# Mixer of the second block: an order of its own for VectorE, and the gates' chain as two events

## What is computed

```python
h = modulate(rms_norm(x, g_norm1), shift1, scale1)
proj = h @ w_in                                # 1024 -> 3088 columns
sb_q, sb_k, sb_v, gq, gk, gv, gg, gf = split(proj)
o_sb = stick_breaking_attention(sb_q, sb_k, sb_v)      # 8 heads of 64
log_alpha = log_sigmoid(gf @ w_fg2 + b_fg2) / 16
o_gla = gla_chunk_causal(gq, gk, gv, log_alpha)        # 4 heads, chunks of 64
o_gla = rms_norm_by_head(o_gla) * g_gla_out * silu(gg)
x = x + (1 + gate1) * (concat(o_sb, o_gla) @ w_out)
```

## Time and profile before

| | |
|---|---|
| median of 3 runs | 1524.2 us (1524.11 to 1524.61) |
| the profiled execution's own time | 1521.82 us |
| its span, first to last instruction | 1520.0 us, mean granted PE clock 0.981 |
| PE busy | 1474.6 us, 97% |
| DVE busy | 785.1 us, 52% |
| ACT busy | 550.4 us, 36% |
| loads of raw weights, 1024 KB each | 5.2 us from issue to landing |
| the mixer | about 851 to 1100 us |

### The profile page before, as it was taken

One profiled execution on the slowest core, in us unless ns is written; L12 is line 12 of the kernel. 1 busy time (PEld: TensorE's weight loads), 2 busy tenths in 40 slices (PEclk: granted clock), 3 DMA queues, 4 the chain that ended last, 5 costly groups with the idle time before them and its releaser, 6 DMA issues.

```text
span 1520.0 us, 18225 instructions
## 1 busy us (share of the span) xinstructions
PE 1474.6 (97%) x6646; PEld 1194.9 (79%) x6646; DVE 785.1 (52%) x1013; ACT 550.4 (36%) x699; POOL 25.2 (2%) x48
## 2 busy tenths in 40 slices
PE   6999999999999999999999888999999999999997
PEld 5887888888888888888888756666677888888886
DVE  7345454566456444544645645454456653563564
ACT  4343212223224422323143514334535542552342
POOL 1000000000000000000000000000000000000000
PEclk8999999999999999999999899999999999999999
DMA  5323544334432334253432211110122232323221
GB/s 174 110 85 119 171 163 155 124 109 169 165 111 83 111 125 152 84 172 103 131 105 83 83 56 56 56 56 28 56 83 83 89 105 83 110 87 107 83 83 55
DMA packets 135789, 158.18 MB, mean 104 GB/s; under 512 B 2513, under 2 KB 129071, under 8 KB 135743
## 3 DMA queue, kind: packets, MB, share of 16 engines
q1 hardware_dynamic: 129024, 131.08, 26.6%
q0 software_dynamic: 6240, 26.30, 5.2%
q10 hardware_dynamic: 479, 0.17, 0.0%
HBM read 155.44 MB, written 2.10 MB: 104 GB/s over the span
## 4 chain that ended last, share of the span: by engine, by line
PE 93%; DVE 3%; ACT 2%; issue 1%; DMA 1%; SPq 0%; ACTq 0%; DVEq 0%
PE bank L437 29%; PE bank L439 28%; PE bank L438 28%; ACT weights_hi L785 1%; PE aux L717 1%; DMA gates<-in_x 1%; PE aux L459 1%; PE aux L741 1%; DVE weights_lo L1116 1%; PE aux L472 1%; PE bank L717 1%; PE aux L652 0%; PE aux L727 0%; PE aux L547 0%; PE aux L506 0%
## 5 line engine op out<-in xcount | busy, mean ns | idle before, releaser
L437 PE MATMUL bank<-operand_hi,weights_hi 128*128 128x512 f32 x1936 | 766.4, 396 | 8.3 <-DVE operand_lo L1128 5.6
L438 PE MATMUL bank<-operand_lo,weights_hi 128*128 128x512 f32 x1936 | 756.8, 391 | 0.0
L439 PE MATMUL bank<-operand_hi,weights_lo 128*128 128x512 f32 x1936 | 756.6, 391 | 0.0
L437 PEld LDWEIGHTS bank<-operand_hi,weights_hi 128*128 128x128 f32 x1936 | 365.8, 189 | 93.4 <-issue 17.5
L439 PEld LDWEIGHTS bank<-operand_hi,weights_lo 128*128 128x128 f32 x1936 | 365.4, 189 | 77.3
L438 PEld LDWEIGHTS bank<-operand_lo,weights_hi 128*128 128x128 f32 x1936 | 366.0, 189 | 75.2 <-issue 1.2
L1116 DVE TENSOR_TENSOR weights_lo<-raw,weights_hi 128x1024 fp32r<-128x1024 f32 (+1 forms) x244 | 296.0, 1214 | 166.9 <-ACT weights_hi L785 161.3
L785 ACT ACTIVATE weights_hi<-raw 128x1024 fp32r<-128x1024 f32 (+1 forms) x244 | 253.6, 1045 | 300.1 <-PE bank L439 300.1
L790 ACT ACTIVATE operand_hi<-value 128x512 f32 (+1 forms) x88 | 55.7, 633 | 125.6 <-DVE value L1304 34.0
L1126 DVE TENSOR_TENSOR operand_lo<-value,operand_hi 128x512 fp32r<-128x512 f32 (+1 forms) x88 | 60.6, 688 | 41.1 <-ACT operand_hi L790 41.1
L1547 DVE SCALAR_TENSOR_TENSOR conv_or_gate<-bank,vector_table,conv_or_gate 128x511 f32<-128x511 f32 x44 | 32.9, 747 | 80.4 <-ACT conv_or_gate L1073 78.5
(11 more groups left out here) (211 smaller groups left out, 695.1 us busy)
## 6 DMA issues: line engine op xcount, KB each, us to landing
raw<-in_w_in SPq DMA_DIRECT2D x40, 1024.0 KB, 5.2
raw<-in_w_ff SPq DMA_DIRECT2D x32, 1024.0 KB, 5.2
ada_or_attention<-in_w_ada POOLq DMA_DIRECT2D x16, 1536.0 KB, 7.6
raw<-in_w_up SPq DMA_DIRECT2D x22, 1024.0 KB, 5.1
raw<-in_w_out SPq DMA_DIRECT2D x8, 1024.0 KB, 5.0
raw<-in_w_down SPq DMA_DIRECT2D x8, 1024.0 KB, 5.0
raw<-in_w_proj_a SPq DMA_DIRECT2D x4, 1024.0 KB, 6.3
raw<-in_w_proj_b SPq DMA_DIRECT2D x4, 1024.0 KB, 6.4
```

The lines of the kernel that those rows point to most:

```text
L437: pe.matmul(dst[:, :], wh, ah, start=(kt == 0), stop=False)
L438: pe.matmul(dst[:, :], wh, al, start=False, stop=False)
L439: mm = pe.matmul(dst[:, :], wl, ah, start=False, stop=(kt == k_tiles - 1))
```

## The change

`vector_order` writes a second list, `VECTOR_MIXER`, from `MIXER`, and only VectorE walks it. It holds a tile's event (its low part and what else VectorE does there) back until the next tile or part begins, and puts the transpositions' copies, the clamps of scores and the two gates' first passes ahead of it; other events (shaping, states, products with k, the heads' scaling) stay behind it. In it the copy of v of tile t stands before the low part at tile t + 1. The gate's event is cut in two: "fg" ends with the logarithm, and a new event "decayed" has VectorE's three sums (`sum_gate`) and ScalarE's two decays. "decayed" 0 stands before tile 7, "decayed" 1 behind the first scores. In `MIXER` itself, for all engines, k_dec, o, ms, turn_gv and the like now stand before the shaping "sp" where both come after the same part. No instruction of arithmetic is added, removed or changed in size.

```diff
--- before.py
+++ after.py
@@ -98,19 +98,22 @@
     order = [("tile", 0)]
     for t in range(1, 4):
         order += [("tile", t), ("turn_v", t - 1)]
-    order += [("tile", 4), ("turn_v", 3), ("fg", 0), ("tile", 5), ("fg", 1), ("tile", 6), ("fg", 2), ("tile", 7)]
+    order += [("tile", 4), ("turn_v", 3), ("fg", 0), ("tile", 5), ("fg", 1), ("tile", 6), ("fg", 2), ("decayed", 0),
+              ("tile", 7)]
     shaped = []
     for t in range(8, 24):
         for part in range(PARTS):
             order.append(("part", (t, part * KT // PARTS, (part + 1) * KT // PARTS)))
+            order += others.get((t, part), [])
             if shaped:
                 order.append(("sp", shaped.pop()))
-            order += others.get((t, part), [])
             step = attend.get((t, part))
             if step is not None:
                 if step < N_ITEMS:
                     order.append(("z", step))
                     shaped.append(step)
+                if step == 0:
+                    order.append(("decayed", 1))
                 if 1 <= step <= N_ITEMS:
                     order.append(("tri", step - 1))
                 if step >= 2:
@@ -120,6 +123,32 @@
 
 
 MIXER = mixer_schedule()
+
+
+def vector_order():
+
+
+
+
+    def ends_tile(event):
+        return event[0] == "tile" or (event[0] == "part" and event[1][2] == KT)
+
+    order, held, late = [], None, []
+    for event in MIXER:
+        if event[0] in ("tile", "part"):
+            if held is not None:
+                order += [held] + late
+            held, late = None, []
+            if ends_tile(event):
+                held = event
+        elif held is None or event[0] in ("turn_v", "turn_k", "turn_gv", "z") or event in (("fg", 1), ("fg", 2)):
+            order.append(event)
+        else:
+            late.append(event)
+    return order + ([held] if held is not None else []) + late
+
+
+VECTOR_MIXER = vector_order()
 
 AUX2 = {e: n for n, e in enumerate(e for e in MIXER if e[0] in ("turn_v", "fg", "turn_k", "turn_gv", "kv", "o", "ms"))}
 
@@ -1023,6 +1052,8 @@
                     act.activation(gate_e[p], gate_e[p], ACT.Exp, scale=-1.0).then_inc(g_exp, 1)
                     act.wait_ge(g_exp, p + 1)
                     act.activation(gate_e[p], gate_e[p], ACT.Ln, bias=one).then_inc(g_log, 1)
+                elif kind == "decayed":
+                    p = n
                     act.wait_ge(g_rest, p + 1)
 
                     act.activation(decay[:, p * NCH:(p + 1) * NCH], gate_e[p][:, CHUNK - 1:S:CHUNK], ACT.Exp,
@@ -1413,6 +1444,10 @@
                 dve.tensor_scalar(y, aux[2][:, :], col(C_BFG + p), -1.0, ALU.add, ALU.mult).then_inc(aux2_read, 1)
                 dve.wait_ge(aux2_read, AUX2[event] + 1)
                 dve.scalar_tensor_tensor(out=e, in0=y, scalar=-1.0, in1=y, op0=ALU.mult, op1=ALU.max).then_inc(g_abs, 1)
+
+            def sum_gate(p):
+
+                y, e = gate_y[p], gate_e[p]
                 dve.wait_ge(g_log, p + 1)
                 dve.scalar_tensor_tensor(out=y, in0=y, scalar=0.0, in1=e, op0=ALU.max, op1=ALU.add).then_inc(g_sp, 1)
                 dve.wait_ge(g_sp, p + 1)
@@ -1424,7 +1459,7 @@
                                   ev[:, :, CHUNK - 1:CHUNK].to_broadcast([P, NCH, CHUNK]), ev,
                                   ALU.subtract).then_inc(g_rest, 1)
 
-            for event in MIXER:
+            for event in VECTOR_MIXER:
                 kind, n = event
                 if kind == "part":
                     if n[2] < KT:
@@ -1459,6 +1494,8 @@
                     dve.tensor_copy(gf_t, aux[2][0:RANK, :]).then_inc(aux2_read, 1)
                 elif kind == "fg":
                     softplus_gate(n - 1, event)
+                elif kind == "decayed":
+                    sum_gate(n)
                 elif kind == "kv":
                     pair, par = n // 2, n % 2
                     dve.wait_ge(aux2_filled, AUX2[event] + 1)
```

## The result

The changed kernel took 1507.1 us (median of 4 runs, 1506.9 to 1508.5) against 1524.15, a ratio of 0.9894 with a 95% interval of 0.9882 to 0.9906. The medians lie 17.0 us apart; the ratio itself stands for 16.2 us (0.0106 of 1524.15). The forecast was 14.8 us less. A later comparison of the same kernels gave 1507.6 against 1523.9, a ratio of 0.9892 (0.9874 to 0.9910).

The account below looks back on a forecast made before the run. TensorE, busy 97% of the span, was taken as the bound. 6.27 + 4.08 + 2.08 - 1.0 + 1.63 + 3.0 - 1.27 = 14.8 us off the median 1524.2 gave 1509.4 us, range 1506.5 to 1515.5.

Parts of the forecast that it names:

- k's transposition: New TensorE wait for the product with k, no longer hidden by TensorE's slowness: cost 1.0 us, bounds 0 and 2.
- copies of v: Waits at the second transposition of v and before the low-rank product shrink or go: 0.87 and 4.17 us won.
- low-rank product's clock: The low-rank product's 24 matmuls, the first six at the lower clock before, take 5.57 instead of 6.80: 1.23 us won.
- The first triangle: TensorE's wait for the mask after the second scores goes, 4.08 us won, and slow clock behind it, 2.08 won.
- The state product: Wait before the fourth head's state product goes, the bank being read before four shaping passes: 1.63 us won, lower bound 1.4.
- slow stretch: Lower clock behind the wait at the fourth head's state product goes: 3.0 us won, bounds 2.4 and 3.4.
- The last triangle: New wait near the mixer's end, last head-norm scaling now ahead of L1501 and mask: cost 1.27 us, bounds 1.0 and 1.6.
- Rival 4: One of the new waits, at k's transposition or the last triangle, doesn't come: 1507 to 1508.5 us; chance 0.07.
- rival 1: The clock falls behind the new waits, each fall costing 1.2 to 3.0: 1510.6 to 1515.4 us; chance 0.20.
- (2): Rival: the gates' split doesn't free the path to the first triangle, gate 1's sums fall on it: 1513.6 us; chance 0.10.
- (3): Rival: low parts at tile ends come too late, TensorE pays per pair of tiles: slower than before; chance 0.05 with the like.

Follow-up runs that it names:

- second experiment: The changed kernel with each gate's sums and decays straight behind its logarithm again, VectorE's own order kept: 1507.6 us.
- first experiment: The changed kernel with VectorE walking the common list again, gates' split and swaps with the shaping kept: 1517.8 us, ratio to before 0.9964.
- run without the three waits: The changed kernel with gates' low-rank product inside tile 5, k's first product before its block's shaping, last shaping before last norm scaling: 1503.9 us.
- single swap: The kernel before with only the third head's scaling out of the bank moved ahead of its block's shaping: 1519.8 us, ratio 0.9977.

## Why the prediction was right, point by point

The mixer cut at five places that both traces have (tile 7, the second scores, k's transposition, the last scores, the next norm's sum), and what each piece lost:

| piece | terms of the sum | forecast | measured |
|---|---|---|---|
| start to tile 7 | copies of v, low-rank product's clock | 6.27 | 6.52 |
| to the second scores | none | 0 | 0.34 |
| to k's transposition | 4.08 + 2.08 - 1.0 | 5.16 | 5.08 |
| to the last scores | 1.63 + 3.0 | 4.63 | 5.16 |
| to the next norm | -1.27 | -1.27 | -1.39 |
| sum | | 14.8 | 15.71 |

**The copies of v.** Right, and additive as the run with them alone shows. After the change DVE waits 2.25 us for PE at the last of them, and the low part comes behind (timeline of DVE; the earlier trace rows had them the other way round):

```profile
886.75 0.69 DVE L1438 COPY kept<-aux 128x512 f32<-128x512 f32 x1 [2.25 <-PE aux L652]
887.89 1.23 DVE L1147 TENSOR_TENSOR weights_lo<-raw,weights_hi 128x1024 fp32r<-128x1024 f32 x1 [0.45 <-ACT weights_hi L814]
```

The 0.8 us of the shortest hand-over stayed, as forecast.

**The first triangle.** The replay (the chain's steps worked through again in the new order) held step by step. Timeline of DVE after, to be read against the earlier trace rows: clamp, three sums of gate 1, L1538, mask; then the next block and k's product:

```profile
915.10 0.95 DVE L1531 TENSOR_SCALAR ada_or_attention<-aux 128x768 f32<-128x768 f32 x1
...
915.97 0.68 DVE L1452 SCALAR_TENSOR_TENSOR under_hi<-under_hi 128x512 f32<-128x512 f32 x1
...
917.94 0.69 DVE L1458 TENSOR_TENSOR under_hi<-under_hi 128x512 f32<-128x512 f32 x1
918.55 0.95 DVE L1538 TENSOR_TENSOR ada_or_attention<-aux,ada_or_attention 128x768 f32<-128x768 f32 x1
919.53 0.69 DVE L1544 TENSOR_TENSOR ada_or_attention<-ada_or_attention,key_before_query 128x512 f32<-128x512 f32 x1
...
924.84 0.96 DVE L1538 TENSOR_TENSOR ada_or_attention<-bank,ada_or_attention 128x768 f32<-128x768 f32 x1 [1.89 <-ACT ada_or_attention L1081]
...
927.34 0.69 DVE L1489 TENSOR_TENSOR under_hi<-mix_bias,under_hi 128x512 f32<-128x512 f32 x1
```

The mixer of this execution starts 2.2 us later than that of before, so the replay's times have to be raised by that: clamp 913.25 forecast, 915.10 - 2.2 = 912.9; mask done 918.6, 920.22 - 2.2 = 918.0; k's product done 926.2, 928.03 - 2.2 = 925.8. All of these are 0.3 to 0.6 early, since PE was early too. But the reason that I gave was too narrow. The sum credited the freed wait to the replay as a whole; the runs show that it had two sufficient causes, and that the gates' split, which the chain in the trace of before points at, earned nothing beside the other. The four traces show how. The first stretch runs from the end of PE's second gate product to the end of DVE's sums, behind which ScalarE makes the decays and then tile 7's evacuation and high part; the second from there to the end of the mask pass:

| kernel | product to sums | sums to mask | mask ends, against the triangle's start |
|---|---|---|---|
| before | 10.9 us | 7.9 us | PE waits 4.1 us |
| own order, gates whole (second experiment) | 6.0 us | 7.9 us | 0.4 us ahead |
| common order, gates split (first experiment) | 5.9 us | 8.5 us | 0.05 us ahead |
| both | 5.2 us | 8.5 us | 0.6 us ahead |

Either part takes some 5 us off the first stretch: the order because the second gate's two passes come right behind its product and not behind a tile's low part, the split because the sums in it are then gate 0's, whose logarithm is long ready. Gate 1's sums, which the split puts between clamp and shaping, cost 0.6 of that. With the split alone the mask comes just in time, so that part had nothing to spare.

**To the second scores, 0.34.** The sum left this out. PE pauses 0.24 us between 922.63 and 923.10 in the kernel before, where matmuls otherwise start 0.23 apart; it is too short to be listed as a wait. Tile 9, which starts there, needs the bank of tile 7, and ScalarE's evacuation of that tile, held behind gate 1's decays, ends at 922.96 (timelines of PE and of ScalarE, before):

```profile
922.63 0.39 PE L439 MATMUL bank<-operand_hi,weights_lo 128*128 128x512 f32 x1
923.10 0.47 PE L437 MATMUL bank<-operand_hi,weights_hi 128*128 128x512 f32 x1
922.38 0.58 ACT L1004 ACTIVATE gates<-bank 128x512 f32<-128x512 f32 x1
```

**k's transposition.** The new wait of 1.0 came, as 1.15, for the reason given: the cover was PE's own slowness. Moving k's product one part forward removes it, as the run without the three waits shows.

**The state product.** The wait went, and with it its slow stretch, as the single swap shows: 4.39 for 4.63 forecast. The reading ahead of the shaping (L1515 now at 1047.04, L1538 behind it) is one way; the run with the shaping first shows that DVE's own order suffices without it. There the clamp starts 1.0 us after PE's scores, against 2.8 before (1052.10 against 1049.27), so the whole block is done earlier. The prediction had named both and didn't say that one would do. From this state product to the last scores PE took 8.91 us before and 5.93 after, so the slow stretch was worth 2.98 for 3.0 forecast. The other 0.5 us of the piece lie almost wholly at the transposition behind k's second, where PE waited 0.2 us for DVE's copy (L1407): from one transposition to the other it took 3.65 us before and 3.21 after. The sum had left that out.

**The last triangle.** Right: L1518 first, L1538 and the mask behind it, done at 1065.69, PE on at 1065.74. From the last scores to this triangle's start PE took 10.68 us before and 11.88 after, 1.20 more for 1.27 forecast; the other 0.19 of the piece lies behind it and isn't placed. The first rows are the state product's, the last three these:

```profile
1047.04 0.75 DVE L1515 TENSOR_SCALAR mix_bias<-aux,vector_table 128x512 f32<-128x512 f32 x1 [2.36 <-ACT evacuated L1066]
1047.70 0.95 DVE L1538 TENSOR_TENSOR ada_or_attention<-aux,ada_or_attention 128x768 f32<-128x768 f32 x1
...
1063.40 0.69 DVE L1518 TENSOR_TENSOR mix_bias<-mix_bias,evacuated 128x512 f32<-128x512 f32 x1 [6.01 <-ACT evacuated L1072]
1064.01 1.22 DVE L1538 TENSOR_TENSOR ada_or_attention<-bank,ada_or_attention 128x1024 f32<-128x1024 f32 x1
1065.27 0.42 DVE L1544 TENSOR_TENSOR ada_or_attention<-ada_or_attention,key_before_query 128x256 f32<-128x256 f32 x1
```

**Rivals.** Rival 4's band, 1507 to 1508.5, holds the measured median, but not for its reason: both new waits came, at 1.15 and 1.04 us, and the time is lower than the 1509.4 forecast through the small terms above and the part outside the mixer. The clock did not fall behind the new waits (rival 1), nor did the sums of gate 1 fall on the path (2): the triangle started the moment the scores were through, 0.6 us after the mask. Low parts came in time everywhere (3). The sentence of the Trainium skill's page TensorE: Matmul & The Clock Gate (A second HAM failure mode) that frequent short idles between groups of matmuls make the clock go back and forth was not borne out by these waits: the window over the stage is at 1.00, though three waits in 254 us may be too few to be called frequent. Where the clock did fall, in the run with 1.3 us ahead of the state product, it was behind a single wait, so no run here bears the sentence out.

**The total.** 17.0 was measured between the medians (16.2 by the ratio, 16.4 in the second comparison), 14.8 forecast, and 15.7 is in the mixer. The remaining 0.5 to 1.3 us are within the interval and no run places them; they may be the scatter of what lies outside the mixer, 2.2 us ahead of the second norm alone.

## What to carry to other kernels

When one list of events drives several engines, the order that suits the producer can make another engine serve slack work (weights wanted four tiles later) while a full bank blocks TensorE: give that engine its own order, urgent bank readings first, and change nothing else. Undo each part by itself before keeping it: here two parts freed the same wait, and a third cost 1.2 us. Undo them together as well, since neither of the two showed its worth alone. Replay the few hand-overs behind a wait with the durations of the rows; that told within 0.2 us which wait would go and which would come, and the two that came could be removed by moving one event each.

## What the runs showed of the hardware

The length of a wait alone doesn't set its price. Ahead of the fourth head's state product the clock fell in all four traces with a wait there: 1.3 us was followed by 6.7 us at 1.2 GHz (3.0 us of time), and 1.6 us by 6.8 us in the kernel before and with the copies of v alone (0.83 from 1050 to 1070 us in both), but by 3.4 with the split alone. Ahead of k's transposition, with 128x512 products around, 1.7 us cost none in two kernels and 3.1 us was followed by 3.4 us of it. The longest wait doesn't bring the longest stretch either: in the kernel before, 5.0 us is followed by 3.4 us at 1.2 GHz (0.83 over 886 to 896 us), and 4.1 us by 6.8 (0.83 over 920 to 940).

Rival 1 of the prediction had gone by length. The place seems to count, but it isn't shown to be the cause: the same 1.6 us at the same product was followed by 3.4 us in one kernel and 6.8 in others, so place and length together don't settle it. The moment at which a wait falls, and what of the surroundings counts, were not tried.
